# Attention in groups of two: values of two groups, then scores of two later ones, in an fp32 transformer kernel

## The reference

```python
def sliding_window_attention(q, k, v, sinks):
    ...
    s = jnp.einsum('bnqkgd,bnskd->bnkgqs', qb, kb,
                   preferred_element_type=jnp.float32) * scale
    ...
    m = jnp.maximum(jnp.max(s, axis=-1, keepdims=True), sink)
    p = jnp.exp(s - m)
    p = p / (jnp.sum(p, axis=-1, keepdims=True) + jnp.exp(sink - m))
    o = jnp.einsum('bnkgqs,bnskd->bnqkgd', p.astype(v.dtype), vb)
```

## Time and profile before

| | us |
|---|---|
| median of 3 runs | 2159.97 |
| lowest and highest | 2159.80, 2160.16 |
| the profiled execution | 2161.53 |
| its span, first to last instruction | 2159.7 |

### The profile page before, as it was taken

The page is one execution under the profiler, slowest core; times in us unless marked ns, Lnnn a source line. Parts: engine busy times, 40 slices in busy tenths (PEclk is TensorE's granted clock), DMA queues, the critical chain, the costliest instruction groups (busy, mean ns, idle before and its releaser), DMA issues.

```text
span 2159.7 us, 29030 instructions
## 1 busy us (share of the span) xinstructions
PE 2148.4 (99%) x10413; PEld 1729.5 (80%) x10413; DVE 1210.7 (56%) x1579; ACT 939.6 (44%) x1515; POOL 1056.6 (49%) x527
## 2 busy tenths in 40 slices
PE   9999999999999999999999999999999999999999
PEld 7877788888888877788888888877787678888887
DVE  7988953222436997864222445859887746333201
ACT  5656533222214656643333215436645655444311
POOL 4962335444444973344444443433766754444442
PEclk9999999999999999999999999999999999999999
DMA  5332223333763332232333572322231112333332
GB/s 183 110 90 69 78 79 107 97 97 97 220 207 89 112 97 69 69 98 88 97 97 97 195 233 78 98 78 69 69 91 56 30 59 87 100 96 97 97 97 87
DMA packets 62869, 219.57 MB, mean 102 GB/s; under 512 B 7936, under 2 KB 8192, under 8 KB 62784
## 3 DMA queue, kind: packets, MB, share of 16 engines
q1 hardware_dynamic: 55296, 191.16, 29.2%
q10 hardware_dynamic: 7488, 27.27, 3.8%
HBM read 212.76 MB, written 2.10 MB: 99 GB/s over the span
## 4 chain that ended last, share of the span: by engine, by line
PE 84%; DVE 8%; ACT 4%; issue 2%; POOL 1%; DMA 0%; SPq 0%; ACTq 0%; POOLq 0%; DVEq 0%
PE bank L1749 26%; PE bank L1751 26%; PE bank L1750 26%; ACT prob L693 1%; DVE row_max L1205 1%; POOL soft_lo L505 1%; DVE conv L1313 1%; DVE row_max L1207 1%; DVE bank L1202 1%; DVE prob_t L1225 1%; ACT wh L561 1%; DVE neg_max L1208 0%; DVE soft_hi L1639 0%; POOL wl L414 0%; PE bank L2248 0%
## 5 line engine op out<-in xcount | busy, mean ns | idle before, releaser
L414 POOL TENSOR_TENSOR wl<-raw,wh 128x1024 fp32r<-128x1024 f32 x349 | 850.0, 2437 | 996.7 <-ACT wh L561 996.7
L1749 PE MATMUL bank<-hh,wh 128*128 128x512 f32 (+1 forms) x1979 | 773.1, 391 | 0.8 <-DVE hl L1449 0.6
L1751 PE MATMUL bank<-hh,wl 128*128 128x512 f32 (+1 forms) x1979 | 763.8, 386 | 0.0
L1750 PE MATMUL bank<-hl,wh 128*128 128x512 f32 (+1 forms) x1979 | 763.2, 386 | 0.0
L561 ACT ACTIVATE wh<-raw 128x1024 fp32r<-128x1024 f32 x351 | 370.1, 1055 | 577.4 <-PE bank L1751 528.2
L1749 PEld LDWEIGHTS bank<-hh,wh 128*128 128x128 f32 x1979 | 372.5, 188 | 81.0 <-issue 7.4
L1751 PEld LDWEIGHTS bank<-hh,wl 128*128 128x128 f32 x1979 | 372.5, 188 | 75.5
L1750 PEld LDWEIGHTS bank<-hl,wh 128*128 128x128 f32 x1979 | 372.7, 188 | 74.3 <-issue 2.2
L1750 PE MATMUL bank<-al,wh 128*128 (+1 forms) x512 | 199.3, 389 | 0.0
L1749 PE MATMUL bank<-ah,wh 128*128 (+1 forms) x512 | 199.3, 389 | 0.0
L1751 PE MATMUL bank<-ah,wl 128*128 (+1 forms) x512 | 199.3, 389 | 0.0
(11 more groups left out here) (389 smaller groups left out, 2722.8 us busy)
## 6 DMA issues: line engine op xcount, KB each, us to landing
raw<-stream SPq DMA_DIRECT2D x351, 512.0 KB, 3.6
ada_w<-ada ACTq DMA_DIRECT2D x48, 512.0 KB, 4.6
x<-x_t ACTq DMA_DIRECT2D x4, 512.0 KB, 7.9
out_t<-x SPq DMA_DIRECT2D x8, 256.0 KB, 2.1
th<-q SPq DMA_DIRECT2D x16, 64.0 KB
th<-q SPq DMA_DIRECT2D x64, 16.0 KB
q<-th SPq DMA_DIRECT2D x16, 64.0 KB, 2.0
cst<-consts SPq DMA_DIRECT2D x1, 640.0 KB, 6.5
```

Of the source, the lines that this page charges most:

```text
L414: nc.gpsimd.tensor_tensor(wl[:, slot, :], raw[:, raw_slot, :], wh[:, slot, :].bitcast(F32), ALU.subtract).then_inc(lo_ready, 1)
L1749: mm(dst, wh[:, slot, w], xh, start=start, stop=False)
L1750: mm(dst, wh[:, slot, w], xl, start=False, stop=False)
L1751: return mm(dst, wl[:, slot, w], xh, start=False, stop=stop)
```

## The change

Groups 2 to 11 are taken by two. In an even step g of the PE, the values of the groups g - 2 and g - 1 come first (in step 2 only those of group 1), and then the scores of g + 2 and g + 3; the transposes and the gate tile follow as before. In the odd steps 3 to 11 there are only the transposes and the tile. Step 12 still makes the values of the groups 10 and 11, and then the scores of 14.

The values of an odd group go to columns 256 to 511 of bank 7, those of an even one to 0 to 255, so that two groups share the bank. The second of two waits only for the copies of the two before. ACT copies both in its loop of the odd group: `attention_out` of the even one waits until the values of both are written.

```diff
+        TWOS_FROM, TWOS_END = 2, 12
...
+        def pv_cols(g):
+            return slice((g % 2) * 2 * P, (g % 2) * 2 * P + 2 * P)
...
                 def attention_out(g):
                     n, j = group(g)
-                    act.wait_ge(pv_ready, 16 * l + g + 1)
+                    first_of_two = g % 2 == 0 and TWOS_FROM <= g < TWOS_END
+                    act.wait_ge(pv_ready, 16 * l + g + (2 if first_of_two else 1))
                     af(q[:, 2 * j:2 * j + 2, n * P:n * P + P],
-                       bank[:, 7, 0:2 * P].rearrange("p (a b) -> p a b", a=2), ACT.Copy).then_inc(pv_out, 1)
+                       bank[:, 7, pv_cols(g)].rearrange("p (a b) -> p a b", a=2), ACT.Copy).then_inc(pv_out, 1)
...
                     if g:
                         gate(g + 3)
-                    attention_out(g)
+                    if g % 2 and g >= TWOS_FROM:
+                        attention_out(g - 1)
+                        attention_out(g)
+                    if g < TWOS_FROM or g >= TWOS_END:
+                        attention_out(g)
...
                     pe.wait_ge(turned_out, 16 * l + g + 1)
                     if g >= 1:
-                        pe.wait_ge(pv_out, 16 * l + g)
+                        second_of_two = g % 2 and TWOS_FROM < g < TWOS_END
+                        pe.wait_ge(pv_out, 16 * l + (g - 1 if second_of_two else g))
+                    cols = pv_cols(g)
...
                 for g in range(16):
                     n, j = group(g)
-                    if g + AHEAD < 16:
-                        scores(g + AHEAD)
-                    if g:
-                        values(g - 1)
+                    if TWOS_FROM <= g < TWOS_END:
+                        if g % 2 == 0:
+                            if g > TWOS_FROM:
+                                values(g - 2)
+                            values(g - 1)
+                            scores(g + AHEAD)
+                            scores(g + 1 + AHEAD)
+                    else:
+                        if g == TWOS_END:
+                            values(g - 2)
+                            values(g - 1)
+                        if g + AHEAD < 16:
+                            scores(g + AHEAD)
+                        if g and g != TWOS_END:
+                            values(g - 1)
```

More of the change, by code:

```diff
@@ L1956, in values @@
                     if g >= 1:
-                        pe.wait_ge(pv_out, 16 * l + g)
+                        second_of_two = g % 2 and TWOS_FROM < g < TWOS_END
+                        pe.wait_ge(pv_out, 16 * l + (g - 1 if second_of_two else g))
+                    cols = pv_cols(g)
                     for kv in range(2):
                         half = slice(HD * kv, HD * kv + HD)
-                        last = mm(bank[half, 7, 0:2 * P], v[:, max(n - 1, 0), half], prob_t[:, g % 2, 0, 2 * kv:2 * kv + 2, :].rearrange("p a b -> p (a b)"),
+                        last = mm(bank[half, 7, cols], v[:, max(n - 1, 0), half], prob_t[:, g % 2, 0, 2 * kv:2 * kv + 2, :].rearrange("p a b -> p (a b)"),
                                   start=True, stop=n == 0)
@@ L1967, in values @@
                             half = slice(HD * kv, HD * kv + HD)
-                            last = mm(bank[half, 7, 0:2 * P], v_step[:, n, half], prob_t[:, g % 2, 1, 2 * kv:2 * kv + 2, :].rearrange("p a b -> p (a b)"),
+                            last = mm(bank[half, 7, cols], v_step[:, n, half], prob_t[:, g % 2, 1, 2 * kv:2 * kv + 2, :].rearrange("p a b -> p (a b)"),
                                       start=False, stop=True)
```

## The result

The changed kernel takes 2171.70 us (median of 6 runs, 2171.20 to 2172.68) against 2159.98 before (6 runs beside them, 2159.80 to 2161.70): 1.0053 times as long, with an interval of 1.0043 to 1.0063. It is 11.7 us slower. The prediction said 2164.4, in a range of 2161.0 to 2166.4: the sign was right, the size was not (4.4 us were forecast), and the time lies outside of the range. The profiled execution took 2171.22 us, 9.7 more than the one of before.

What follows compares the result with a forecast made beforehand. The prediction took PE, busy 99% of the span, as the bound. A layer: -1.98 + 3.14 + 0.6 - 1.04 = +0.72, +2.22 with the clock; two layers +4.4 us, giving 2164.4 us, range 2161.0 to 2166.4.

Steps and rivals of the forecast that it cites:

- Part 1: Steps 3 to 12: fewer changes of matmul shape among scores (S), values (V) and transposes (T), -1.98 us a layer.
- the 0.81 of S(5): PE time of group 5's scores, 0.81 us, taken over by step 2 from step 3.
- Part 2: Step 2: group 5's scores start 2.5 us late, waiting for group 3's exponentials; +3.14 us a layer net.
- the 0.46 of step 3: Shape changes that step 3 no longer pays, holding only transposes and a tile: 0.46 us.
- Part 3: Later steps: group 13's scores newly wait 0.6 us for group 11's exponentials; two earlier waits go, -1.04 us.
- The old waits: PE's waits in the values of groups 11 and 12, 0.56 and 0.48 us, expected to go: -1.04 us a layer.
- Part 4: TensorE's clock falls to half for 3.4 us at step 2 in each layer: +1.5 us a layer, bounds 0 and 1.7.
- The sum: All terms: +0.72 us a layer, +2.22 with the clock, +4.4 for two layers, forecast 2164.4 us.
- the later PE makes other pairs wait: Rival: longer clock fall, or scores of later groups wait for exponentials; another 1.0 to 1.7 us a layer, chance 0.10.

Runs made afterwards that it cites:

- the kernel with the pair moved: Changed kernel with DVE's normalising multiplies of the convolution and two silu multiplies moved behind the next loop's gate multiply: 2166.14 us.
- step 2 alone: Changed kernel with the group of two kept only at step 2, every group from 4 on by itself: 2168.18 us.
- without step 2: Changed kernel with groups taken by two only from step 4 on: 2165.43 us, in three heaps.
- The kernel before with the pair moved: Kernel before the change, PE's order untouched, with DVE's normalising multiplies of the convolution and two silu multiplies moved behind the next step's gate multiply: 2158.67 us.
- both stalls filled: Changed kernel with unused matmuls in PE's new waits, 11 in step 2 and 10 in step 10: 2166.72 us.
- idle work in step 2: Changed kernel with 11 unused matmuls between the scores of groups 4 and 5 in step 2: 2169.76 us.

## Where the prediction was right and where it was wrong

**Part 1 (shapes, -1.98 a layer): right but for 0.16.** T in an odd step stands 0.23 behind the last matmul of the tile (159.06 to 159.29 in the changed kernel), and S(13) in the kernel with the pair moved stands 0.65 behind S(12). The price of a change holds, but the sum counts one of 0.16 twice, in the 0.81 of S(5) that part 2 takes off and in the 0.46 of step 3 (shown by the run with step 2 alone). Values by two and scores single save 0.73 us a layer beside the same kernel without it (96.88 to 96.15), and 5 x 0.15 = 0.75 was the estimate.

**Part 2 (step 2, +3.14): right** in its starts, each within 0.04 us.

**Part 3 is the step that failed:** "The exponentials of 11 ended at 213.12 + 0.20 = 213.32, and their chain is now up to 0.3 late, as its gate multiplies follow later tiles: a new wait of 0.4 to 0.7, taken as 0.6." They ended at 217.95, 4.63 late. I had seen the link (DVE's gate multiply waits for a tile) and sized it by the time that DVE had to spare before, and left out that an even step now does the scores and values of two groups: T(8) is 201.16 - 196.24 = 4.9 late, the tile behind it too, and the multiply at 207.33 waits 1.16 us for it. T(9), after an odd step with little in it, is only 3.4 late. So PE comes to S(13) early by its odd steps, and DVE and ACT come late by the even ones. Behind the multiply stand two gating multiplies, normalise, the pair of 3.49 us, the mask and the maxima, in a chain with nothing to spare, so nothing was made up. PE could have gone at 215.52, only 2.5 later than the 213.0 of the sum, so the wait was 218.01 - 215.52 = 2.49 and not 0.6. It is no product of step 2 or of the clock: without step 2 and without a fall S(13) waits as long. The same chain held up V(9) (0.29), and the shorter odd step showed the variance's wait (0.59) ahead of the tile of step 7; neither was in the sum. The move of the pair shows that these waits hang on that chain: S(13)'s is gone with it. The old waits did go, and were worth 1.35 from start to start and not the 1.04 of idle time: V(11)'s second half stood 1.22 behind its first where 0.48 is the work, and lost 0.05 more at its restart, and V(12) stood 0.56 too late. The kernel before with the pair moved has neither and gains 98.24 - 96.88 = 1.36. But they went not because PE is late by itself: with step 2 alone it is late too, and 0.8 of the listed 1.04 stay. What took their place is the wait of S(13), ahead of them.

**Part 4 (clock, +1.5): right in the cause, a little small in price**, 1.61 instead of 1.5, and wrong in one thing: I took a fall as something that the place either has or not. It differs between executions of one program, and between its two layers.

**The sum.** For the first layer 2.22 was forecast and 103.24 - 98.24 = 5.00 measured, 2.78 more. From start to start the differences are 1.89 for S(13), 0.59 for the variance, 0.29 for V(9), 0.16 for the change counted twice and 0.13 for the clock (7.60 us from T(2) to T(3), where the kernel with step 2 alone has 5.97 without a fall); 0.31 went the other way in the old waits. That makes 2.75. Two layers are 5.6 us too little. The rest of 2171.7 - 2164.4 = 7.3, 1.7 us, is about one more fall, past the attention: the forecast was set against a median of before without one, and the profiled run of the changed kernel has it at 1339.7. That the other runs have it too is an estimate: even the fastest of them, at 2171.2, equals the 2166.4 us of the runs with both stalls filled and a full clock, plus three falls of 1.6. The rival "the later PE makes other pairs wait" was the right one and had S(9) and S(11) in it, which don't wait; it had a chance of 0.10, and even its upper end of 2167.8 is 3.9 us too low.

## What to carry to other kernels

When an engine's queue is regrouped, the engines that it feeds don't move with its mean but with its latest block: take, for each new wait, the chain that ends it, follow that chain back over one whole step to where it last waited for the engine being changed, and shift it by the delay of that place. Here grouping paid only for work whose inputs had long been there, so group what reads finished data (here the values) and leave single what gives buffers back to a chain (here the scores). If a chain of small operations binds, look first at what its engine does beside a neighbour that can hold it up: moving a few multiplies by half a step gave 1.3 us a layer, the values by two 0.3 alone and 0.7 with the move.

## What the runs showed of the hardware

- A vector operation with both inputs in SBUF stood still beside POOL's 128x1024 operation until that was over, at either size tried: 128x8 as a pair took 2.43 us instead of 0.24, 128x512 as a pair 3.49 instead of 1.28. Operations that read a bank ran beside the same POOL work at their usual 0.69.
- After the same stall of 2.4 us at the same place of a program TensorE's clock fell from 2.4 to 1.2 GHz in one layer and not in the other. A fall lasted 3.4 us each time and cost 1.61 (step 2 alone), 1.60 (idle work in step 2) and 1.38 us (pair moved, where it began at 150.7, before the stall ended at 150.96). The runs of one kernel stand in heaps that go with the mean clock, 3.0 us apart for the kernel without step 2 (1.00, 0.998, 0.997).
- Idle matmuls in the stall, 10 or 11 of 0.23 us each, kept the clock at 1.00 in both attentions and gave back what the falls there cost, 1.6 us a layer. With only the first stall filled, a fall came at the other in one of the two layers.
